# TensorE products into an unread PSUM bank ahead of four kinds of wait in a two-layer hybrid decoder step

## The chip, the cores and the metric

One NeuronCore of a Trainium2 chip runs the whole program. The metric is the time of one execution in microseconds (us); for the kernel before it is the median of three runs. A profile was taken of one further execution.

## The reference, cut to what matters

The program computes one step of a two-layer decoder trunk for 512 prompt tokens and 8 sequences of 4 sample tokens, 544 columns in all, with a model width of 1024. Layer 0 has an HGRN2 mixer (gated linear recurrence), layer 1 a gated DeltaNet mixer with a causal convolution over four taps; a squared-ReLU MLP of width 4096 follows each. Everything is float32. Of layer 1, which the change touches:

```python
q = l2norm(q) * DK ** -0.5; k = l2norm(k)
beta = sigmoid(b); g = -exp(A_log) * softplus(a + dt_bias)
M = eye + where(strict, beta * kk * decay, 0)          # a unit lower triangle per chunk
u = triangular_solve(M, v * beta); w = triangular_solve(M, k * (beta * exp(G)))
# then, chunk by chunk: v_new = u - w S; o = qg S + (qk * decay) v_new; S = gl S + kd^T v_new
```

The dense projections around it are `h @ w_in` and `o @ w_out`. Nothing in the reference answers to the products that the change adds.

## The kernel before, in words

**Layout.** Activations are held transposed, features on 128 partitions, tokens along the free axis, in eight tiles of 128 x 544 (`xT`). A dense projection is a chain of "units": a unit multiplies eight 128 x 128 weight tiles by eight activation tiles. Each of its eight steps (`tiles`, line 494) issues six products of 272 columns, since weight and activation are split into a high and a low part of type float32r and three of the four cross terms are kept; they go to the PSUM tensor `pj`. All other TensorE work is in plain float32 and goes to `rr`, a PSUM tensor of four banks: transposes (`tr`, line 541), sums over features by a matrix of ones (`sum_features`, line 523, two products of 128 x 272) and the recurrence itself.

**Order of the work.** Each engine runs one program in its own order and waits on semaphores. TensorE (PE) has no other order than the one written out in the block from line 490 on. The first mixer, its output projection and its MLP come first. Then the second mixer begins with a prologue: `first_unit(U_AB, "n2")` projects the 16 gate columns, `gdn_pre` (line 684) waits for VectorE and ScalarE to turn them into decay factors and transposes the result (line 689), and the loop at line 941 walks the list `GDN_SLOTS` for head 0: `more(n)` (from `head_projections`, line 513) issues n steps of that head's four projection units, then `gdn_prepare(slot, 0)` issues the small products of the slot. 16 steps go ahead of slot L0 and two ahead of each slot in `GDN_FILLED`, until all 32 are used, which is the case from slot L5 on. Slot L5 (line 718) sums the squares of k, L6 (721) forms k k^T, C0 (727) sums the squares of q, C1 (731) forms k q^T and C2 (737) transposes three small columns. Each of them waits for VectorE or ScalarE. `gdn_first_inverse` (line 744) transposes the first inverse; then 16 steps of the next head's projections follow (line 945).

**The heads.** `gdn_rec` (line 761) runs once for each of eight heads. It builds the inverse of M by doubling: for m = 2, 4, ..., 64 it forms a product `x{m}` (line 783 for m = 2, else line 787), waits for ScalarE's copy of it, forms `dt{m}` (line 823), waits for VectorE to put that in place (`pred{m}`, line 2062), transposes the result (`tr{m}`, line 833, counted under line 543) and waits for ScalarE's copy `tt{m}` (line 1385) before the next level. Steps of the next head's projections (`more`) and its slots are put between these. At m = 16 the wait for `tt8` stands at line 778, right behind slot L3 of the next head (line 715). VectorE's own list there is long: three convolution taps (line 1881), a negative absolute value (1665) and the decay of the sample states (1654) lie ahead of `pred16`. Head 7 prepares no next head. Heads are counted from 0.

Of the kernel before, what the change touches and what calls it, by code (L numbers as in the profile page):

```python
# [14 lines left out]
P = 128  # L15
# [6 lines left out]
HALF = T // 2  # L22
# [113 lines left out]
def fixed(eng, value):  # L136

    return value if isinstance(value, int) else eng.to_reg(value)


def build(nc, x_prompt, x_sample, state_hgrn, state_gdn, state_conv, norm_mix, norm_mlp, norm_final, hgrn_w_in,
          hgrn_lb, hgrn_out_norm, hgrn_w_out, gdn_w_in, gdn_conv_w, gdn_A_log, gdn_dt_bias, gdn_out_norm, gdn_w_out,
          mlp_w_up, mlp_w_down, const_f, const_u, y_prompt, y_sample, hgrn_p, hgrn_s, gdn_p, gdn_s, conv_p, conv_s):
    with ExitStack() as ctx:
        def sb(name, shape, dt=F32):
            return ctx.enter_context(nc.sbuf_tensor(name, shape, dt))
# [5 lines left out]
        xT = sb("xT", [P, KT, T])  # L152
# [13 lines left out]
        ones = sb("ones", [P, P])  # L166
# [61 lines left out]
        rr = ctx.enter_context(nc.psum_tensor("rr", [P, 4, 512], F32))  # L228
# [262 lines left out]
        def _(pe):  # L491
            mm = nc.tensor.matmul
# [30 lines left out]
            def sum_features(bank, src, start=True, stop=True):  # L523

                for b in range(2):
                    last = mm(rr[:, bank + b, 0:HALF], ones[:], src[:, b * HALF:(b + 1) * HALF], start=start, stop=stop)  # L526
                return last
# [13 lines left out]
            def tr(out, in_):  # L541
                n = in_.shape[0]
                return nc.tensor.transpose(out, in_, cf[0:n, C_EYE:C_EYE + n])  # L543
# [63 lines left out]
            def hgrn_rec(h, more):  # L607
# [73 lines left out]
                t.did(sum_features(2, hg["sq"]), "ss")  # L681
                more(3)

            def gdn_pre():
                v, s, t = st["gp"]
                pe.wait_ge(v.sem, v.after("turn", 0))
                pe.wait_ge(s.sem, s.after("eg", 0))
                for c in range(NC):
                    tr(rr[:, 2, c * P:(c + 1) * P], gt4[:, c * P:(c + 1) * P])
                t.did(tr(rr[0:TS, 3, 0:P], gt4[:, TP:T]), "cols")  # L690

            def held(*waits):

                values = [(steps.sem, fixed(pe, steps.after(name, h))) for steps, name, h in waits]
                pe.wait_ge(c_in, 16 * N_CONST)
                for sem_, value in values:
                    pe.wait_ge(sem_, value)

            def gdn_prepare(slot, h):

                v, s, t = st["ga"]
                nQ, nK, work = gd["nQ"], gd["nK"], gd["work"]
                if slot == "L1":
                    loaded = fixed(pe, h * 16 + 16)
                    pe.wait_ge(c_in, 16 * N_CONST)
                    pe.wait_ge(cv_in, loaded)
                    for g in range(3):
                        last = tr(rr[:, 3, SVN + g * 32:SVN + g * 32 + XW * NSEQ], cin[:, g, :])
                    t.did(last, "cin")
                if slot in ("L3", "L4"):  # L710
                    g, name = (0, "gb") if slot == "L3" else (1, "bb")
                    pe.wait_ge(s.sem, s.after("G" if g else "hist", h))
                    pe.wait_ge(v.sem, v.after("gsel", h))
                    for b in range(2):
                        last = mm(rr[:, 2 + b, 0:HALF], ones[32 * g:32 * (g + 1), :],
                                  work[32 * g:32 * (g + 1), b * HALF:(b + 1) * HALF], start=True, stop=True)
                    t.did(last, name)
                if slot == "L5":
                    pe.wait_ge(s.sem, s.after("sqk", h))
                    t.did(sum_features(2, work), "ssk")  # L720
                if slot == "L6":
                    pe.wait_ge(v.sem, v.after("kb", h))
                    for c in range(NC):
                        cols = slice(c * P, (c + 1) * P)
                        mm(rr[:, 2 + c // 2, c % 2 * P:(c % 2 + 1) * P], nK[:, cols], work[:, cols], start=True, stop=True)  # L725
                    t.did(mm(rr[0:TS, 2, 2 * P:2 * P + TS], nK[:, TP:T], work[:, TP:T], start=True, stop=True), "kk")
                if slot == "C0":
                    pe.wait_ge(s.sem, s.after("sqq", h))
                    pe.wait_ge(v.sem, v.after("kkd", h))
                    t.did(sum_features(2, gd["G"]), "ssq")  # L730
                if slot == "C1":
                    pe.wait_ge(v.sem, v.after("qn", h))
                    for c in range(NC):
                        cols = slice(c * P, (c + 1) * P)
                        mm(rr[:, 2 + c // 2, c % 2 * P:(c % 2 + 1) * P], nK[:, cols], nQ[:, cols], start=True, stop=True)  # L735
                    t.did(mm(rr[0:TS, 3, 2 * P:2 * P + TS], nK[:, TP:T], nQ[:, TP:T], start=True, stop=True), "qk")
                if slot == "C2":
                    held((v, "qkd", h))
                    for g in range(3):
                        n = XW * (NSEQ + 1)  # L740
                        last = tr(rr[0:n, 2 + g // 2, g % 2 * P:(g % 2 + 1) * P], cstash[:, g, :])
                    t.did(last, "stash")
# [12 lines left out]
            def gdn_finish(h):  # L755

                _, s, t = st["gf"]
                pe.wait_ge(st["gr"][1].sem, st["gr"][1].after("sq", h))
                t.did(sum_features(2, gd["sq"]), "ss")

            def gdn_rec(h, prev, nxt, more, later):
# [3 lines left out]
                K, qe, A, NL, Tm, Tt, X, kdT, vT, VN = (gd[n] for n in ("K", "qe", "A", "NL", "Tm", "Tt", "X", "kdT",  # L765
                                                                        "vT", "VN"))


                for n, m in enumerate(LEVELS[1:]):
                    smp = m in SLEVELS  # L770
                    if n == 0:
                        pe.wait_ge(sa.sem, sa.after("tm0", h))
                        if prev is not None:
                            pe.wait_ge(v.sem, v.after("sn1", prev))
                        if prev is not None:
                            gdn_finish(prev)
                    else:
                        pe.wait_ge(s.sem, s.after(f"tt{LEVELS[n]}", h))
                    if n == 0:
                        for c in range(NC):  # L780
# [3 lines left out]
                    else:  # L784
                        pe.wait_ge(mixed.sem, mixed.after(f"m{m}", h))
                        for q in range(NC // 2):
                            last = mm(rr[:, 0, q * P:(q + 1) * P], NLm[n % 2][:, q * P:(q + 1) * P], earlier(Tm, q, m),  # L787
                                      start=True, stop=True)
                    if smp:
                        last = mm(rr[0:TS, 1, 0:TS // 2], NL[0:TS, TP:T], first_half(Tm[0:TS, TP:T], m),  # L790
                                  start=True, stop=True)
                    t.did(last, f"x{m}")
                    if m == 4 and nxt is not None:
                        pe.wait_ge(v.sem, v.after("vb", h))
                        gdn_prepare("L1", nxt)
                    if m == 32 and nxt is not None:
                        held((s, "rs", h))
                        gdn_prepare("L4", nxt)
                    if m == 64 and nxt is not None:
                        held((s, "vns", h))  # L800
                        gdn_prepare("L5", nxt)
# [23 lines left out]
                    if smp:  # L825
                        last = mm(rr[0:TS, 1, TS // 2:TS], Tt[0:TS, TP:T], X[0:TS, TP // 2:T // 2],
                                  start=True, stop=True)
# [37 lines left out]
                for q in range(NC // 2):  # L865
                    last = mm(rr[:, 0, 256 + q * P:256 + (q + 1) * P], X[:, q * P:(q + 1) * P], later_ends(Tt, q),
                              start=True, stop=True)
# [68 lines left out]
            mlp(U_MLP0, "n1", "up0")  # L936
            first_unit(U_AB, "n2")
            gdn_pre()
            more = head_projections(U_GIN, 0)
            pe.wait_ge(st["gp"][1].sem, st["gp"][1].after("cols", 0))  # L940
# [3 lines left out]
            gdn_first_inverse(0, (st["ga"][1], "cout", 0))  # L944
            head_projections(U_GIN, 1, 0, 2)(2 * KT)
            gdn_rec(0, None, 1, head_projections(U_GIN, 1, 2, 4), head_projections(U_GIN, 2, 0, 2))
            with pe.Fori(1, H - 2) as h:
                gdn_rec(h, h - 1, h + 1, head_projections(U_GIN, h + 1, 2, 4), head_projections(U_GIN, h + 2, 0, 2))
# [5 lines left out]
            def first_two(n):  # L954
                n = min(n, (6 if n == 1 else 12) - taken[0])
                more(n)
                taken[0] += n

            gdn_rec(H - 2, H - 3, H - 1, head_projections(U_GIN, H - 1, 2, 4), first_two)
            held_back = [28]  # L960

# [530 lines left out]
        def _(dve):  # L1492
# [36 lines left out]
            for i in (0, 2):  # L1529
                after(t, "t", i)  # L1530
                v.did(cp(xT[:, :, i * P:(i + 1) * P], rr[:, 2:4, :].rearrange("p a (k n) -> p (a k) n", n=P)), "copy")
            v2, _, t2 = st["xs"]
            after(t2, "t", 0)
            v2.did(cp(xT[:, :, TP:T], rr[:, 2, 0:KT * TS].rearrange("p (k n) -> p k n", n=TS)), "copy")
# [324 lines left out]
            def gdn_prepare(slot, h):  # L1859
# [27 lines left out]
                def silu(name, row, dst):  # L1887

                    after(s, f"{name}sig", h)
                    for (o, a), (_, b) in list(zip(by_position(dst, pr[:, row, 0:T]), by_position(dst, ng[:, row, 0:T])))[0:2]:  # L1890
                        tt(o, a, b, ALU.mult)
                    v.did(tt(blocks(dst[:, TP:T], SLEN), blocks(pr[:, row, SB0:XPW], SROW)[:, :, 0:SLEN],
                             blocks(ng[:, row, SB0:XPW], SROW)[:, :, 0:SLEN], ALU.mult), f"{name}s")
# [353 lines left out]
```

## Time and profile before

| | us |
|---|---|
| median of 3 runs | 1838.19 |
| lowest and highest run | 1837.34, 1839.09 |
| the profiled execution | 1838.72 |
| its span, first to last instruction | 1836.9 |
| mean granted TensorE clock in the span | 0.959 of full speed |

In the profile, PE is TensorE's matmul side and PEld its weight loads; DVE is VectorE, ACT ScalarE, POOL GpSimd. A granted clock of 1.00 is the 2.4 GHz level, 0.50 the 1.2 GHz level. The end of a product is modelled and includes the time in which it drains, so products issued back to back overlap in the rows: their spacing is shorter than the length of one. A row of the timeline joins instructions of one line that follow each other; the bracket at its end is the idle time of the engine ahead of it and the instruction that ended it.

### The profile page before, as it was taken

To read this page: it belongs to the slowest core of one execution; us is meant where nothing else is said; L and a number is where in the kernel's file an instruction comes from. 1 tells how busy PE (TensorE), PEld (TensorE's weight loads), DVE (VectorE), ACT (ScalarE), POOL (GpSimd) and SP (SyncE) were. 2 spreads that over 40 slices of the span, in tenths; PEclk is the share of its full clock that TensorE was granted. 3 is DMA by queue.
4 is the path that set the end of the run, shared out by engine and by line. 5 is a ranking of instruction groups with operands and counts; after the bars stand their busy time and mean duration, and the time that the engine had idled before them with its cause. 6 is when DMAs were issued, how large, how long until landed. Compare 5 with 4: busy or idle time off the path is not lost.

```text
span 1836.9 us, 33057 instructions
## 1 busy us (share of the span) xinstructions
PE 1704.1 (93%) x12555; PEld 1606.0 (87%) x12555; DVE 1101.8 (60%) x2177; ACT 700.0 (38%) x1220; POOL 38.8 (2%) x85
## 2 busy tenths in 40 slices
PE   6999999899999999977998998999898999999996
PEld 6988888899999999976887787777777999999996
DVE  5888888865343443556568667766765434344444
ACT  5555555543122222224345445444533312122222
POOL 0000000000000000000100100000010000000000
PEclk9999999999999999988899998999998999999997
DMA  5232222223323233221121221121122223323321
GB/s 167 63 89 81 70 81 70 77 84 92 88 86 92 82 89 92 70 69 36 48 61 36 60 60 35 48 60 48 35 75 65 84 85 89 92 81 91 90 70 49
DMA packets 257849, 135.07 MB, mean 74 GB/s; under 512 B 6746, under 2 KB 256180, under 8 KB 257780
## 3 DMA queue, kind: packets, MB, share of 16 engines
q1 hardware_dynamic: 219920, 113.35, 22.0%
q10 hardware_dynamic: 37860, 20.76, 3.9%
q8 instruction: 49, 0.80, 0.2%
q14 instruction: 20, 0.16, 0.0%
HBM read 122.09 MB, written 12.00 MB: 73 GB/s over the span
## 4 chain that ended last, share of the span: by engine, by line
PE 42%; DVE 6%; issue 3%; ACT 2%; ACTq 0%; DVEq 0%
PE pj L505 31%; PE rr L543 3%; PE rr L526 1%; DVE pr L1881 1%; PE rr L787 1%; PE rr L807 1%; PE rr L823 1%; PE rr L895 1%; DVE w_lo L1540 1%; DVE ws L2062 0%; ACT ng L1245 0%; DVE ws L1648 0%; PE rr L725 0%; PE rr L735 0%; DVE ng L1665 0%
## 5 line engine op out<-in xcount | busy, mean ns | idle before, releaser
L505 PE MATMUL pj<-xh,w_hi 128*128 128x272 f32 x2064 | 461.6, 306 | 23.4 <-DVE w_lo L1540 13.0
L1017 ACT ACTIVATE w_hi<-w_raw 128x1024 fp32r<-128x1024 f32 x211 | 222.4, 1054 | 581.9 <-PE pj L505 565.3
L505 PE MATMUL pj<-xh,w_lo 128*128 128x272 f32 x2064 | 434.8, 293 | 0.0
L505 PE MATMUL pj<-xl,w_hi 128*128 128x272 f32 x2064 | 434.6, 293 | 0.0
L505 PEld LDWEIGHTS pj<-xh,w_hi 128*128 128x128 f32 x2064 | 330.7, 194 | 52.8 <-issue 29.5
L505 PEld LDWEIGHTS pj<-xl,w_hi 128*128 128x128 f32 x2064 | 333.1, 193 | 0.0
L505 PEld LDWEIGHTS pj<-xh,w_lo 128*128 128x128 f32 x2064 | 331.3, 194 | 0.0
L1540 DVE TENSOR_TENSOR w_lo<-w_raw,w_hi 128x1024 fp32r<-128x1024 f32 x211 | 256.8, 1217 | 41.1 <-ACT w_hi L1017 41.0
L505 PE MATMUL pj<-oh,w_hi 128*128 128x272 f32 x1254 | 266.6, 294 | 14.6 <-DVE w_lo L1540 10.4
L505 PE MATMUL pj<-oh,w_lo 128*128 128x272 f32 x1254 | 262.1, 291 | 0.0
L505 PE MATMUL pj<-ol,w_hi 128*128 128x272 f32 x1254 | 261.3, 290 | 0.0
L505 PEld LDWEIGHTS pj<-oh,w_hi 128*128 128x128 f32 x1254 | 199.5, 191 | 18.9 <-DVE w_lo L1540 11.5
L505 PEld LDWEIGHTS pj<-ol,w_hi 128*128 128x128 f32 x1254 | 200.0, 191 | 0.0
L505 PEld LDWEIGHTS pj<-oh,w_lo 128*128 128x128 f32 x1254 | 198.5, 191 | 0.0
L2153 DVE TENSOR_TENSOR ws<-pj,rstd 128x544 f32<-128x544 f32 x64 | 46.4, 724 | 188.2 <-PE pj L505 180.0
L2165 DVE TENSOR_TENSOR xT<-xT,pj 128x544 f32<-128x544 f32 x48 | 34.6, 721 | 167.9 <-PE pj L505 167.9
L543 PE MATMUL rr<-cf,ws 128*128 128x128 f32 (+2 forms) x440 | 73.3, 306 | 21.2 <-DVE ws L2062 10.8
L543 PEld LDWEIGHTS rr<-cf,ws 128*128 128x128 f32 (+2 forms) x440 | 53.6, 152 | 35.4 <-DVE ws L2062 14.0
L482 POOL COPY ws<-ws 128x128 f32<-128x128 f32 x80 | 38.4, 513 | 1327.2 <-DVE ws L1968 872.1
L1881 DVE SCALAR_TENSOR_TENSOR pr<-xp,hcw,pr 128x568 f32<-128x568 f32 x72 | 58.2, 809 | 7.3 <-ACT pr L1240 5.8
L1669 DVE SCALAR_TENSOR_TENSOR ng<-pr,ng 128x544 f32<-128x544 f32 (+1 forms) x56 | 40.6, 726 | 32.1 <-ACT ng L1105 19.0
L526 PE MATMUL rr<-ws,ones 128*128 128x272 f32 x148 | 44.4, 424 | 11.6 <-ACT ws L1295 3.8
(317 smaller groups left out, 1959.9 us busy)
## 6 DMA issues: line engine op xcount, KB each, us to landing
w_raw<-in_mlp_w_up_dram SPq DMA_DIRECT2D x64, 512.0 KB, 4.1
w_raw<-in_mlp_w_down_dram SPq DMA_DIRECT2D x64, 512.0 KB, 3.9
w_raw<-in_hgrn_w_in_dram SPq DMA_DIRECT2D x32, 512.0 KB, 4.2
w_raw<-in_gdn_w_in_dram SPq DMA_DIRECT2D x32, 512.0 KB, 4.0
out_dram<-S ACTq DMA_DIRECT2D x16, 512.0 KB, 3.3
S<-in_state_hgrn_dram ACTq DMA_DIRECT2D x8, 512.0 KB, 4.1
w_raw<-in_hgrn_w_out_dram SPq DMA_DIRECT2D x8, 512.0 KB, 3.8
S<-in_state_gdn_dram ACTq DMA_DIRECT2D x8, 512.0 KB, 4.0
```

The source lines that it names most:

```text
L482: last = nc.gpsimd.tensor_copy(interleaved(NLm[n % 2], m, odd), pair_half(gd["NL"][:, 0:TP], m, odd, odd))
L505: last = mm(pj[:, s, b, 0:HALF], w[:, s, k, :], v[:, k, b * HALF:(b + 1) * HALF], start=(k == 0 and a == 0), stop=(k == end - 1 and a == 2))
L526: last = mm(rr[:, bank + b, 0:HALF], ones[:], src[:, b * HALF:(b + 1) * HALF], start=start, stop=stop)
L543: return nc.tensor.transpose(out, in_, cf[0:n, C_EYE:C_EYE + n])
L787: last = mm(rr[:, 0, q * P:(q + 1) * P], NLm[n % 2][:, q * P:(q + 1) * P], earlier(Tm, q, m), start=True, stop=True)
L807: last = mm(rr[:, 1, 2 * b * SLEN:2 * (b + 1) * SLEN], S0[:, b, :], both, start=True, stop=True)
L1017: f(w_hi[:, c % SPLIT, 0:n], w_raw[:, slot, 0:n], ACT.Copy).then_inc(w_high, 1)
L1540: tt(w_lo[:, c % SPLIT, 0:n], w_raw[:, c % RAW, 0:n], w_hi[:, c % SPLIT, 0:n], ALU.subtract).then_inc(w_low, 1)
L1669: return stt(out=ng[:, row, 0:w], in0=pr[:, row, 0:w], scalar=0.0, in1=ng[:, row, 0:w], op0=ALU.min, op1=ALU.subtract)
L1881: v.did(stt(out=pr[:, row, 0:YW], in0=xp[:, row, j:j + YW], scalar=hcw[:, j, g:g + 1], in1=pr[:, row, 0:YW], op0=ALU.mult, op1=ALU.add), f ...
L2153: tt(halves(B[:, k % 2]), computed(U, r, k), halves(rstd[:]), ALU.mult).then_inc(unit_out, 1)
L2165: tt(halves(xT[:, k]), halves(xT[:, k]), computed(U, g * (2 * KT), KT + k), ALU.add).then_inc(unit_out, 1)
```

## The change

It adds a helper `keep_busy`, which issues n float32 products of the matrix of ones with a source that lies ready, each of which starts and stops its own accumulation in a given bank of `rr`. No instruction reads what they write. It is called at four kinds of place on PE: in `gdn_pre` ahead of the two waits (44 products of 272 columns, bank 3); in the prologue's slots L5, L6 and C1, of head 0 alone (16, 12 and 8 products of 272 columns, bank 0); and in each of the eight heads at level m = 16, ahead of the wait for `tt8` (4 products of 256 columns, bank 0). No other engine's program changes, and no wait or DMA is added or moved.

```diff
+            def keep_busy(bank, src, n):
+
+                for _ in range(n):
+                    mm(rr[:, bank, 0:src.shape[1]], ones[:], src, start=True, stop=True)
+
             def gdn_pre():
                 v, s, t = st["gp"]
+                keep_busy(3, xT[:, 0, 0:HALF], 44)
                 pe.wait_ge(v.sem, v.after("turn", 0))
                 pe.wait_ge(s.sem, s.after("eg", 0))
...
                 nQ, nK, work = gd["nQ"], gd["nK"], gd["work"]
+                if isinstance(h, int) and h == 0 and slot in ("L5", "L6", "C1"):
+                    keep_busy(0, xT[:, 0, 0:HALF], 16 if slot == "L5" else 12 if slot == "L6" else 8)
                 if slot == "L1":
...
                     else:
+                        if m == 16:
+                            keep_busy(0, A[:, 0:2 * P], 4)
                         pe.wait_ge(s.sem, s.after(f"tt{LEVELS[n]}", h))
```

## Rows read from the trace of the kernel before

**Rows 1.** The page, span in 40 slices: granted clock in tenths of full speed.
```profile
PEclk9999999999999999988899998999998999999997
```
**Rows 2.** Stretches of set length: busy time (instructions) per engine, granted clock, DMA share, GB/s.
```profile
810.80:824.40 13.60, 5.46 (x23) 5.01 (x24) 4.99 (x10) 3.99 (x11) 0.00 (x0) 0.50 0.15 39
...
855.20:879.00 23.80, 14.42 (x51) 10.85 (x52) 16.90 (x41) 12.48 (x23) 1.22 (x4) 0.50 0.18 47
974.70:978.00 3.30, 3.30 (x17) 3.30 (x17) 3.19 (x5) 1.46 (x3) 1.05 (x2) 0.50 0.00 0
...
1107.80:1114.50 6.70, 5.27 (x25) 4.88 (x24) 5.27 (x14) 2.61 (x8) 0.64 (x1) 0.50 0.00 0
...
1305.80:1309.00 3.20, 0.76 (x7) 0.55 (x5) 3.13 (x7) 0.31 (x1) 0.21 (x1) 1.00 0.00 0
1309.20:1312.50 3.30, 3.30 (x15) 3.07 (x15) 1.89 (x9) 2.23 (x6) 0.00 (x0) 0.50 0.00 0
```
**Rows 3.** Timeline of PE, 805 to 825 us: start, us, line, operation, count, [idle before, releaser].
```profile
805.77 1.08 PE L526 MATMUL rr<-ws,ones 128*128 128x272 f32 x4
...
807.19 0.42 PE L505 MATMUL pj<-xh,w_lo 128*128 128x272 f32 x2
818.50 1.30 PE L543 MATMUL rr<-cf,gt 128*128 128x128 f32 x5 [10.89 <-ACT gt L1221]
820.23 0.82 PE L505 MATMUL pj<-xh,w_hi 128*128 128x272 f32 x2 [0.43 <-ACT gcol L1224]
```
**Rows 4.** Timeline of PE, 851 to 880 us.
```profile
851.61 0.41 PE L505 MATMUL pj<-xh,w_lo 128*128 128x272 f32 x2
855.78 2.18 PE L526 MATMUL rr<-ws,ones 128*128 128x272 f32 x4 [3.76 <-ACT ws L1295]
861.36 2.08 PE L725 MATMUL rr<-ws 128*128 128x128 f32 x8 [3.40 <-DVE ws L1941]
...
869.05 2.08 PE L735 MATMUL rr<-ws 128*128 128x128 f32 x8 [2.25 <-DVE ws L1953]
...
874.37 1.28 PE L543 MATMUL rr<-cf,ws 128*128 128x128 f32 x5 [1.20 <-DVE ws L1982]
875.58 0.82 PE L505 MATMUL pj<-xh,w_hi 128*128 128x272 f32 x2
```
**Rows 5.** PE's waits, 880 to 1440 us: total us, times, longest.
```profile
PE rr L787 <- ACT ws L1385: 10.7, 7, 1.6
...
PE rr L787 <- DVE rt L2093: 0.6, 1, 0.6
```
**Rows 6.** Timeline of PE around level 16, heads 1 (from 971) and 6 (from 1301).
```profile
971.55 1.18 PE L715 MATMUL rr<-ws,ones 32*128 32x272 f32 x4
974.28 0.94 PE L787 MATMUL rr<-ws 128*128 128x128 f32 x4 [1.56 <-ACT ws L1385]
...
979.48 0.66 PE L543 MATMUL rr<-cf,ws 128*128 128x128 f32 x4 [0.97 <-DVE ws L2062]
...
980.83 0.40 PE L787 MATMUL rr<-ws 128*128 128x128 f32 x2
...
1303.90 0.71 PE L787 MATMUL rr<-ws 128*128 128x128 f32 x4 [1.48 <-ACT ws L1385]
...
1306.15 0.41 PE L505 MATMUL pj<-xh,w_lo 128*128 128x272 f32 x2
1309.09 1.11 PE L543 MATMUL rr<-cf,ws 128*128 128x128 f32 x4 [2.52 <-DVE ws L2062]
...
1311.58 0.84 PE L787 MATMUL rr<-ws 128*128 128x128 f32 x3
```
**Rows 7.** The chain that ended last, in order of time, head 0 around level 16.
```profile
911.15 0.82 DVE pr L1881
...
912.66 1.22 DVE S L1654
```
**Rows 8.** The instructions of line 526: duration ns min/median/max, first and last start.
```profile
L526 PE MATMUL rr<-ws,ones x148: 390/393/821, 31.5 to 1814.6; 128*128 128x272 f32 x148
```

## The prediction

> **What bounds the kernel now.** I read the page's clock line first, then stretches of set length, then PE's timeline and waits where the clock is low, then the chain that ended last.
>
> The clock line is at 9 or more but for the second mixer [rows 1]. There the half level (0.50) holds for 13.6 us around the gates' wait and for 23.8 us at the end of the prologue, and once or twice in each head [rows 2]. Ahead of the first stretch PE idles 10.89 us for the gates, and its projections then start at the half level at 820.23 [rows 3]. Ahead of the second it idles 3.76 us for the squares of k, then 3.40 and 2.25 us [rows 4]. In the heads, `x16` waits some 1.5 us for `tt8` in heads 0 to 6, together 10.7 us, and 0.6 us in head 7 [rows 5]. The reader is to see two sorts of low clock: one where PE's products are next on the path (the prologue's projections), and one where another engine is. At level 16 the chain runs through VectorE's taps of 0.82 us and the decay of 1.22 us, not through PE [rows 7].
>
> **One added product.** The nearest row is the same instruction: `sum_features` has two calls of 128 x 272 float32, and its row has four matmuls, 1.08 us in all [rows 3]. So a call is two records. The last one is 0.39 long [rows 8], so the spacing is (1.08 - 0.39) / 3 = 0.23 us, and a call takes 0.46 us at the full level. One of 256 columns takes 0.46 x 256/272 = 0.43. At the half level four records take 2.18 [rows 4], twice as much.
>
> **The gates' wait.** 44 calls take 44 x 0.46 = 20.2 us. They begin behind the last projection step (807.19 + 0.42, its drain aside, 807.4) and end at 827.6. Today the transposes start at 818.50, so PE comes 9.1 us late. Gained: the five transposes go at the full level, 0.65 instead of 1.30, so the projections start at 828.7 instead of 820.23, 8.5 us later. Today they run at the half level from 820.23 to 824.4 [rows 2, 3]; these 4.2 us would be 2.1. Behind them all engines wait for PE's first unit (VectorE is busy 4.99 of 13.60 us there [rows 2], all of it ahead of the wait), so nothing hides the delay. Net **+6.4**; bounds +5.4 (a gap between transposes and projections that shrinks) and +8.5 (nothing regained). ScalarE and VectorE stand still meanwhile, and SyncE's weight loads behind them, which nobody needs earlier.
>
> **The prologue's three slots.** L5: 16 calls, 7.3 us, begin at 852.0 and end at 859.3 instead of 855.78, 3.5 us late; the sum at the full level takes 1.1 us less, lag 2.4. L6: 12 calls, 5.5 us, against a wait of 3.40: lag 2.4 + 2.1 = 4.5, less 1.2 for k k^T at the full level, 3.3. The next sum has no calls ahead of it and takes 1.1 less, lag 2.2. C1: 8 calls, 3.7 us, against 2.25: lag 3.6, less 1.2 for k q^T, 2.4. VectorE's work up to 874.37 is as long as before. The transposes there take 0.64 less and the 3.4 us of projections up to 879.0 that ran at the half level take 1.7 less: lag 0.1. But in the last 3 us ahead of the projections PE is left with three short transposes. Head 6 shows what follows: 0.76 us busy of 3.2 at the full level, then 3.3 us at the half level [rows 2]. I take the same here, 1.6 lost. Net **+1.7**; bounds 0 and +3.4 (two such stretches).
>
> **The heads.** Four calls take 1.73 us and end where `x16` starts now (behind the sums from 971.55 they end at 974.3; it starts at 974.28 [rows 6]). In heads 0 to 6 that is no delay, and 0.1 us would be hidden behind VectorE's taps. In head 7 the calls overrun a wait of 0.6 us [rows 5] plus a drain of some 0.15: **+1.0** (bounds 0 and 1.0).
>
> What does the clock give back there? Head 1 goes from `x16` to the transposes of `pred16` in 979.48 - 974.28 = 5.20 us with 3.3 of them at the half level; head 6 in 1309.09 - 1303.90 = 5.19 at the full level [rows 2, 6]. Nothing: VectorE ends last. But from the transposes to `x32` head 1 (full) takes 980.83 - 979.48 = 1.35 and head 6 (half) 1311.58 - 1309.09 = 2.49. A low stretch is free while VectorE works and costs 1.1 us once it comes later. Calls ahead of `x16` take away the first idle time, but the second stays: behind `dt16` PE waits 2.52 us in head 6 [rows 6]. So the low stretch doesn't go in all heads; in some it moves from the free place to the dear one. Heads 3 (low from 1107.8 to 1114.5 [rows 2]) and 6 pay already. I take two more of the other five, **+2.0**; bounds -2.2 (heads 3 and 6 freed too) and +5.5 (all five).
>
> The Trainium skill says otherwise (TensorE: Matmul & The Clock Gate, section on HAM oscillation): a throttled stretch costs its length times 1 - 1.2/2.4, so half of it. By that each of seven heads would gain at least 1.6 us here. Heads 1 and 6, equal within 0.01 us, do not bear it out at this place.
>
> **The sum.** 6.4 + 1.7 + 1.0 + 2.0 = 11.1 us on the profiled execution of 1838.72, which is 0.5 above the median: 1849.3 as a median. What this measurement can tell from no change is about 0.2%, 3.7 us.
>
> **The rivals.**
>
> *The low stretches simply go*, in heads 3 and 6 too, and none comes back ahead of the next head's projections: 6.4 + 0 + 1.0 - 2.2 = 5.2, 1843.4. For it: the calls are back to back. Against: the second idle time at level 16. Chance 0.15.
>
> *The low stretches move to the dear place in all heads* and stay for twice the time in the prologue: 6.4 + 3.4 + 1.0 + 5.5 = 16.3, 1854.5. Chance 0.15.
>
> *The half level costs half its time everywhere, and the change is faster.* The stretches aimed at are 13.6 + 23.8 us and, with one per head like those of heads 1, 3 and 6, about 27 in seven heads: 64 us, so 32 gained. Against that stand PE's overruns at full speed: 9.1 + 3.5 + 2.1 + 1.4 + 1.0 = 17.1. That is 15 us faster, 1823. It decides as soon as more than 17.1 of the 32 are on the path; by the sums above it is 2.8 at the gates, some 6 in the slots and at most 2.2 in the heads. Chance 0.07. It is the rule of the Trainium skill named above, carried through.
>
> *The change does not do what it says*: a call is one record, 0.23 us. Then 44 calls (10.1 us) and the slots' 3.7, 2.8 and 1.8 fit into 10.89, 3.76, 3.40 and 2.25; the gates gain 2.8 and the slots some 6: 1829. The count of the four matmuls speaks against it [rows 3]. Chance 0.03.
>
> *The overrun at the gates is swallowed* by a wait that I don't see, and the rest cancels: 1838 to 1841. Chance 0.05.
>
> **How the numbers follow.** The forecast has 0.55 and is 1849.3. All low bounds give 5.4 + 0 + 0 - 2.2 = 3.2, all high ones 8.5 + 3.4 + 1.0 + 5.5 = 18.4; with the cases of 1843.4 and 1854.5 inside, the range is 1842 to 1857. Faster: 0.07 + 0.03 = 0.10; same 0.05; slower 0.85.
>
> **What would show it.** The added line under the gates should show 88 matmuls over some 20 us, the transposes of line 543 at about 827.6 with no idle time ahead of them, the wait for ScalarE there gone, and the clock at 1.00 from 807 on. The sum of line 526 in the prologue should start about 3.5 us later relative to the work ahead of it and take 1.08. In heads 0 to 6 the distance from `x16` to the transposes of `pred16` should stay 5.2 us, and PE's wait on line 2062 there grow to some 2.5 us. Transposes at 818 to 819 us would make the forecast wrong at its largest term; a distance well under 5.2 us would make the reading of the heads wrong; a low clock right behind the 44 calls would mean that such products do not hold it.

## The result, and the profile after

The median is 1850.03 us (1845.17 to 1851.22, five runs) against 1838.19 (1836.86 to 1841.49): the ratio that the runs give is 1.0055 (the two medians alone give 1.0064), with a 95% interval of 1.0041 to 1.0070, so 0.4 to 0.7% slower. The profiled execution took 1850.03, its span 1848.2 us. The mean granted clock rose from 0.959 to 0.972, and the time rose too. Below, a "low stretch" is a time in which the granted clock is 0.50.

The page's clock line has lost the run of eights at the prologue that [rows 1] show:

```profile
PEclk9999999999999999999999999998998999999997
```

PE's timeline at the gates' wait answers to [rows 3] (start, us, line, operation, count, idle before and its releaser; the added products are line 687):

```profile
807.59 20.33 PE L687 MATMUL rr<-xT,ones 128*128 128x272 f32 x88
...
827.76 0.71 PE L543 MATMUL rr<-cf,gt 128*128 128x128 f32 x5
...
828.90 0.52 PE L505 MATMUL pj<-xh,w_hi 128*128 128x272 f32 x2 [0.43 <-ACT gcol L1234]
```

The 44 calls are 88 matmuls, as the count of four for two calls had said, one every (827.76 - 807.59) / 88 = 0.23 us. The wait for ScalarE of 10.89 us has no row any more: when PE comes to it, the gates are long ready. The transposes begin 9.3 us later than in [rows 3], the projections 8.7; 0.14 us of each is the start of the norm's sum, 805.91 against 805.77.

The end of the prologue, same view, answers to [rows 4]:

```profile
858.63 7.49 PE L687 MATMUL rr<-xT,ones 128*128 128x272 f32 x32
...
865.96 1.08 PE L526 MATMUL rr<-ws,ones 128*128 128x272 f32 x4
866.88 5.66 PE L687 MATMUL rr<-xT,ones 128*128 128x272 f32 x24
872.38 1.05 PE L733 MATMUL rr<-ws 128*128 128x128 f32 x8
...
875.56 3.83 PE L687 MATMUL rr<-xT,ones 128*128 128x272 f32 x16
879.23 1.05 PE L743 MATMUL rr<-ws 128*128 128x128 f32 x8
...
883.43 1.27 PE L543 MATMUL rr<-cf,ws 128*128 128x128 f32 x5 [1.52 <-DVE ws L1992]
884.64 0.82 PE L505 MATMUL pj<-xh,w_hi 128*128 128x272 f32 x2
```

The sum of slot L5 and the products of L6 and C1 now take half as long (1.08, 1.05 and 1.05 us) and have no idle time ahead of them, but each starts late. Behind the last of them PE idles again, the last transposes take 1.27 us, as long as before, and the projections at 884.64 start with a length of 0.82, the half level's. Stretches of set length show the clock there (busy time and instructions of PE, PEld, DVE, ACT, POOL; granted clock; DMA share; GB/s), as [rows 2] did:

```profile
807.60:827.70 20.10, 20.10 (x90) 16.67 (x89) 7.43 (x14) 5.49 (x13) 0.00 (x0) 1.00 0.12 34
858.70:882.80 24.10, 21.29 (x104) 17.47 (x102) 17.11 (x38) 13.85 (x25) 0.68 (x3) 1.00 0.12 27
882.90:889.60 6.70, 6.17 (x27) 5.77 (x28) 3.13 (x15) 1.76 (x4) 0.44 (x2) 0.50 0.23 66
```

In the heads, PE's timeline around level 16 of head 1, and behind it the late part of head 5, answer to [rows 6]:

```profile
982.24 1.18 PE L723 MATMUL rr<-ws,ones 32*128 32x272 f32 x4
983.35 1.99 PE L687 MATMUL rr<-ws,ones 128*128 128x256 f32 x8
985.18 0.61 PE L797 MATMUL rr<-ws 128*128 128x128 f32 x4
...
990.09 0.66 PE L543 MATMUL rr<-cf,ws 128*128 128x128 f32 x4 [2.36 <-DVE ws L2072]
...
991.44 0.62 PE L797 MATMUL rr<-ws 128*128 128x128 f32 x4
...
1254.93 1.05 PE L797 MATMUL rr<-ws 128*128 128x128 f32 x4
1255.92 2.18 PE L723 MATMUL rr<-ws,ones 32*128 32x272 f32 x4
...
1263.48 0.61 PE L797 MATMUL rr<-ws 128*128 128x128 f32 x4
```

Head 1 goes through level 16 at the full level. Its `x16` comes 0.2 us later behind the start of the sums than in [rows 6] (985.18 - 982.24 = 2.94 against 2.73), and from there it is 4.91 us to the transposes instead of 5.20: what is lost ahead of `x16` is idle time less behind it, and the idle time ahead of the transposes has grown from 0.97 to 2.36. In head 5 the low clock comes where it hurts: from `x32` at 1254.93 to `x64` at 1263.48 are 8.55 us, against 6.1 in heads that keep the clock. PE was busy in all of that low stretch:

```profile
1255.00:1261.70 6.70, 6.70 (x25) 5.53 (x25) 3.84 (x10) 5.54 (x12) 0.00 (x0) 0.50 0.25 73
```

Where the time went can be read off three starts in PE's timeline: the norm's sum of line 526 ahead of the gates (805.77 before, 805.91 after), `x2` of head 0 (889.25; 899.04) and `x2` of head 7 (1347.72; 1358.08), and from there to the second sample update `dSs1` of head 7. The same three distances are given for every kernel below; "prologue" is from the norm to head 0.

| kernel | median, us | ratio to before, interval | profiled execution | prologue | heads 0-6 | head 7 |
|---|---|---|---|---|---|---|
| before | 1838.19 | | 1838.72 | 83.48 | 458.47 | 44.01 |
| the change | 1850.03 | 1.0055 (1.0041 to 1.0070) | 1850.03 | 93.12 | 459.04 | 44.89 |
| gates only, 44 | 1842.76 | 1.0033 (1.0019 to 1.0047) | 1841.30 | 90.23 | 454.97 | 43.99 |
| slots only | 1839.20 | 1.0011 (0.9998 to 1.0024) | 1844.43 | 86.56 | 459.31 | 43.98 |
| heads only | 1840.10 | 1.0013 (1.0002 to 1.0024) | 1836.00 | 84.16 | 455.75 | 44.90 |
| gates only, 23 | 1835.96 | 0.9998 (0.9985 to 1.0010) | 1836.93 | 81.14 | 457.62 | 44.00 |
| slots fitted | 1836.95 | 0.9999 (0.9988 to 1.0010) | 1835.69 | 80.85 | 457.37 | 44.00 |
| slots covered | 1836.60 | 0.9986 (0.9975 to 0.9998) | 1836.71 | 79.64 | 459.38 | 43.99 |
| heads, two fills | 1836.26 | 0.9990 (0.9979 to 1.0002) | 1836.56 | 83.69 | 455.05 | 43.99 |
| all fitted | 1831.84 | 0.9964 (0.9949 to 0.9979) | 1827.47 | 77.91 | 451.92 | 44.01 |

The ratios go by runs on the experiment's own chip, where the kernel before had medians of 1837.57 (30 runs) and 1837.78 (34), with single runs from 1832.2 to 1841.7. The three parts of the change, 1.0033, 1.0011 and 1.0013, add up to 1.0057 there, against 1.0055 for the whole. But such a spread hides a part of 2 us, so the parts are read from the three distances as well, each from one profiled execution. Head 7 repeats best, 43.98 to 44.01 in the eight kernels that leave it alone; the prologue is 83.48, 83.69 and 84.16 in the three that leave it alone; heads 0 to 6 vary most, and the next section shows why. The profiled execution can lie anywhere among the runs: with the slots only it was the slowest of twelve, with the heads only it was 4 us below its median. Up to 1.8 us of the difference between two such executions lies outside the three distances, where the kernels do not differ.

### The profile page after: what moved, and what is told of

The parts are those of the page before. It is cut to its first block, busy times and chain, and to the rows that moved or that the text cites. A ratio compares the mean times of both kernels' runs of the same rounds, so it can differ in the third digit from the quotient of the medians.

```text
span 1848.2 us, 33505 instructions
## 1 busy us (share of the span) xinstructions
PE 1739.5 (94%) x12779; PEld 1637.7 (89%) x12779; DVE 1102.2 (60%) x2177; ACT 700.6 (38%) x1220; POOL 37.2 (2%) x85
## 4 chain that ended last, share of the span: by engine, by line
PE 80%; DVE 11%; issue 4%; ACT 4%; ACTq 0%; DVEq 0%; DMA 0%
PE pj L505 61%; PE rr L543 4%; PE rr L687 2%; PE rr L526 2%; DVE w_lo L1550 2%; PE rr L623 1%; DVE pr L1891 1%; PE rr L668 1%; PE rr L661 1%; PE rr L797 1%; PE rr L817 1%; PE rr L833 1%; PE rr L905 1%; DVE ws L1581 1%; PE rr L743 0%
## 5 line engine op out<-in xcount | busy, mean ns | idle before, releaser
L1444 ACT ACTIVATE oh<-ws 128x544 fp32r<-128x544 f32 x64 | 42.3, 661 | 28.9 <-DVE ws L2165 28.9
```

Of the source, the lines that this page charges most:

```text
L1444: s.did(f(oh[:, k], B[:, 2 + k % 2], ACT.Copy), f"hi{k}")
```

## The experiments

**Gates only.** The change without its calls in the slots and the heads.

```diff
-                if isinstance(h, int) and h == 0 and slot in ("L5", "L6", "C1"):
-                    keep_busy(0, xT[:, 0, 0:HALF], 16 if slot == "L5" else 12 if slot == "L6" else 8)
-                        if m == 16:
-                            keep_busy(0, A[:, 0:2 * P], 4)
```

> Only the 44 products at the gates' wait. Overrun theory: the added products end at 827.8, 9.2 us after the gates are ready; with the clock kept at 1.00 the net is +6.6 us, so 6 to 7 us over the kernel before. Rival (half-level time costs half of itself, the overrun is swallowed by slack behind it): the low stretch of 13.6 us goes and 2 to 7 us are gained.

Measured: prologue +6.75 us, ratio 1.0033, so +6 us. The overrun is paid in full. It is read best where PE next waits for weights, in the kernel before and here:

```profile
836.47 0.52 PE L505 MATMUL pj<-xh,w_hi 128*128 128x272 f32 x2 [2.08 <-DVE w_lo L1540]
...
842.50 0.52 PE L505 MATMUL pj<-xh,w_hi 128*128 128x272 f32 x2 [2.08 <-DVE w_lo L1546]
```

Behind the norm's sum (805.77 before, 805.14 here) that is 30.70 us and 37.36, so 6.66 us later, and VectorE has moved with PE: the wait for it is 2.08 us in both. In the whole change the distance is 37.36 as well. Behind this place the present kernel has a low stretch of 3.4 us that the whole change lacks; its 1.3 us come back in shorter waits and in the next low stretch but for 0.1.

**Slots only.** The change without its calls at the gates and in the heads.

```diff
-                keep_busy(3, xT[:, 0, 0:HALF], 44)
-                        if m == 16:
-                            keep_busy(0, A[:, 0:2 * P], 4)
```

> Only the 16, 12 and 8 products in the slots L5, L6 and C1 of the prologue. Overrun theory: between +0.1 us, if the clock stays up behind C1, and +3.4 us, if PE's projections of the next head run at the half level for two stretches as they did with the whole change; I take +3. Rival (half of the 23.8 us of low clock is gained, less 7 us of overrun): 5 us faster than the kernel before.

Measured: prologue +3.08 us. The long low stretch ahead of the next head's projections goes from 23.9 us to 6.8, and this part still loses: all three groups overrun their waits, and the stretch that is left lies on the next head's projections. With the gates the two parts make 6.75 + 3.08 = 9.83, against 9.64 for the whole change. The median's +2 us is no contradiction, its interval reaches from -0.4 to +4.4.

**Heads only.** The change without its calls at the gates and in the slots.

```diff
-                keep_busy(3, xT[:, 0, 0:HALF], 44)
-                if isinstance(h, int) and h == 0 and slot in ("L5", "L6", "C1"):
-                    keep_busy(0, xT[:, 0, 0:HALF], 16 if slot == "L5" else 12 if slot == "L6" else 8)
```

> Only the 4 products at level 16 of each head. Theory (VectorE ends last at level 16, and a low stretch costs only where it falls behind pred16): head 7 pays 0.9 us, the others between -2 and +4 us together depending on where the low stretches fall; 0 to +4 us. Rival (each low stretch of 3.4 us at level 16 costs half of it): four to seven of them go and 7 to 12 us are gained, less 0.9.

Measured: head 7 +0.89 us, ratio 1.0013. None of the seven other heads has a low stretch at level 16; head 4 has one of 6.8 us from `x32` on instead, and takes 67.58 us where it took 65.27 before. In this execution heads 0 to 6 are 2.7 us shorter than before, but the runs have the part as a whole 0.4 to 4.4 us slower. This and the kernel with the gates only make the cleanest pair of the study, for in the latter a low stretch begins around `x16` and ends ahead of `pred16` in each of heads 0 to 6. PE around level 16 of head 1 with the gates only (`x16` is line 793), and the clock there:

```profile
980.43 1.22 PE L793 MATMUL rr<-ws 128*128 128x128 f32 x4 [1.56 <-ACT ws L1391]
...
985.54 0.66 PE L543 MATMUL rr<-cf,ws 128*128 128x128 f32 x4 [0.88 <-DVE ws L2068]
...
986.90 0.62 PE L793 MATMUL rr<-ws 128*128 128x128 f32 x4
```
```profile
980.50:983.80 3.30, 3.30 (x15) 3.30 (x16) 3.19 (x5) 1.46 (x3) 1.54 (x2) 0.50 0.00 0
```

and the same head with the heads' calls only (`x16` is line 794):

```profile
973.95 0.61 PE L794 MATMUL rr<-ws 128*128 128x128 f32 x4
...
978.87 0.66 PE L543 MATMUL rr<-cf,ws 128*128 128x128 f32 x4 [2.36 <-DVE ws L2069]
...
980.22 0.61 PE L794 MATMUL rr<-ws 128*128 128x128 f32 x4
```
```profile
970.00:981.00 11.00, 8.64 (x57) 7.35 (x56) 9.83 (x23) 4.79 (x13) 1.10 (x2) 1.00 0.00 0
```

`x16` takes 1.22 us in the one and 0.61 in the other, and the head as a whole, from `x2` to the next `x2`, takes 65.25 us in both. Heads 0, 3, 5 and 6 agree within 0.02 us too; heads 2 and 4 differ by longer low stretches elsewhere. PE at double speed buys idle time: 2.36 us ahead of the transposes instead of 0.88, both released by VectorE's `pred16`. Half of a low stretch is not what it costs here; nothing is.

**The gates' wait, filled but not overrun.** 23 calls instead of 44, nothing else.

```diff
-                keep_busy(3, xT[:, 0, 0:HALF], 44)
+                keep_busy(3, xT[:, 0, 0:HALF], 23)
```

> Only the gates, with 23 products instead of 44: 46 matmuls of 0.229 us, 10.5 us, which fit into the 10.9 us wait. Overrun theory: the transposes start at 818.5 as before, go at the full level, and the projections start at 819.7 and run at the full level: 2.4 to 2.8 us faster than the kernel before. If something else held the prologue (the rival in which the overrun is swallowed), this would change nothing, 0 within 1 us.

PE's timeline at the gates (no row lies between the first two), where it next waits for weights, and the clock behind that:

```profile
808.48 10.71 PE L687 MATMUL rr<-xT,ones 128*128 128x272 f32 x46
819.54 0.74 PE L543 MATMUL rr<-cf,gt 128*128 128x128 f32 x5 [0.35 <-ACT gt L1227]
...
835.10 0.52 PE L505 MATMUL pj<-xh,w_hi 128*128 128x272 f32 x2 [2.08 <-DVE w_lo L1546]
```
```profile
836.20:839.50 3.30, 3.30 (x17) 3.00 (x16) 0.00 (x0) 0.95 (x6) 0.00 (x0) 0.50 0.59 160
```

Measured: prologue -2.34 us. The five transposes take 0.74 us instead of 1.30, the projections behind them run at the full level, and the wait for weights ends 28.30 us behind the norm's sum (806.80), 2.40 earlier than before. That is what the gates give. Behind it lies a low stretch that the kernel before does not have there. It costs PE 1.3 us; 0.65 of that is made up by a shorter wait for ScalarE ahead of L5, and 0.6 because the next low stretch ends earlier against the projections, so that the -2.34 of the whole prologue agrees partly by chance. 21 calls more, at 0.46 us each, are 9.6 us; less the 0.35 us that is idle here they make 9.3, and the two prologues differ by 9.1. The median is 1.6 us below the one of before, and the runs alone could not tell this from no change.

**The slots, fitted.** 8, 9 and 5 calls instead of 16, 12 and 8, nothing else.

```diff
-                    keep_busy(0, xT[:, 0, 0:HALF], 16 if slot == "L5" else 12 if slot == "L6" else 8)
+                    keep_busy(0, xT[:, 0, 0:HALF], {'L5': 8, 'L6': 9, 'C1': 5}[slot])
```

> Only the slots, with 8, 9 and 5 products instead of 16, 12 and 8, so that they end before the waits do. Theory: nothing is late any more; k k^T and the sum of the squares of q at the full level give 1.1 us each, the wait of k k^T itself stays (VectorE's taps end last there), and the projections behind still start at the half level: from the gates' norm to x2 of head 0 about 81.3 us against 83.5 before, so 2 us faster. Rival (half of the low clock counts): the 23.8 us of low clock give 8 to 10 us.

Measured: prologue -2.63 us, 80.85 against the 81.3 expected; the median -0.8, within the interval. The end of the prologue, and the clock ahead of and behind its last transposes:

```profile
870.65 0.49 PE L543 MATMUL rr<-cf,cstash 128*27 128x128 f32 x3 [1.97 <-DVE ws L1907]
872.66 1.27 PE L543 MATMUL rr<-cf,ws 128*128 128x128 f32 x5 [1.52 <-DVE ws L1989]
873.87 0.82 PE L505 MATMUL pj<-xh,w_hi 128*128 128x272 f32 x2
```
```profile
868.60:872.40 3.80, 0.57 (x5) 0.24 (x3) 3.70 (x11) 1.85 (x4) 1.05 (x4) 1.00 0.25 47
872.50:875.80 3.30, 3.14 (x13) 2.75 (x14) 2.77 (x14) 1.76 (x4) 0.07 (x1) 0.50 0.37 106
```

PE is busy 0.57 of 3.80 us, and the half level follows, onto the projections.

**The slots, fitted and covered.** The same, with products ahead of three more waits.

```diff
-                    keep_busy(0, xT[:, 0, 0:HALF], {'L5': 8, 'L6': 9, 'C1': 5}[slot])
+                    keep_busy(0, xT[:, 0, 0:HALF], {'L5': 8, 'L6': 9, 'C0': 2, 'C1': 5, 'C2': 4}[slot])
...
+                if isinstance(h, int) and h == 0:
+                    keep_busy(0, xT[:, 0, 0:HALF], 3)
                 pe.wait_ge(v.sem, v.after("tt1", h))
```

> As the fitted slots, and 2 products ahead of C0's wait, 4 ahead of C2's and 3 ahead of the first inverse's, so that no idle time is left ahead of the next head's projections. Theory: these now run at the full level: from the norm to x2 about 79.2 us against 83.5 before, 2 us less than with the fitted slots alone; 4 us faster than the kernel before. If the low stretch came for another reason than the idle time ahead of it, it would stay and this would equal the fitted slots.

The last transposes, the first projections and the clock in the same place:

```profile
873.40 0.79 PE L543 MATMUL rr<-cf,ws 128*128 128x128 f32 x5
874.12 0.52 PE L505 MATMUL pj<-xh,w_hi 128*128 128x272 f32 x2
```
```profile
868.60:872.40 3.80, 3.80 (x22) 2.94 (x22) 3.77 (x9) 1.80 (x4) 0.31 (x2) 1.00 0.11 14
873.00:885.00 12.00, 11.85 (x94) 11.39 (x92) 5.00 (x19) 2.82 (x5) 0.31 (x2) 1.00 0.18 43
```

Measured: prologue -3.84 us, ratio 0.9986. No low stretch is left at the end of the prologue. The 3.3 us of half level in the fitted slots were worth 80.85 - 79.64 = 1.2 us; here PE is next, and the larger part of half their length is really paid.

**Two fills in the heads.** The 4 products at level 16, in heads 0 to 6 alone, and 5 more ahead of the wait for `pred16`, in bank 1, whose last content ScalarE has copied by then.

```diff
-                        if m == 16:
+                        if m == 16 and nxt is not None:
                             keep_busy(0, A[:, 0:2 * P], 4)
...
                     more(1)
+                    if m == 16 and nxt is not None:
+                        keep_busy(1, A[:, 0:2 * P], 5)
                     pe.wait_ge(v.sem, v.after(f"pred{m}", h))
```

> Only heads 0 to 6: the 4 products ahead of tt8 and 5 more (bank 1) ahead of the wait for pred16, where PE was idle for 2.5 us. Theory: no low stretch at level 16 in any head, so x32 always comes 1.36 us behind the transposes of pred16, and heads 0 to 6 take 453.4 us plus 1.5 for each long low stretch at dSs0, about 455 against 458.5 in the profile of before; 2 to 4 us faster than it, 0 to 3 in the median. Rival (half of each stretch counts): 7 x 1.7 = 12 us faster.

PE in head 1 from the second fill to `x32`:

```profile
977.65 2.32 PE L687 MATMUL rr<-ws,ones 128*128 128x256 f32 x10
980.16 0.66 PE L543 MATMUL rr<-cf,ws 128*128 128x128 f32 x4 [0.19 <-DVE ws L2071]
...
981.51 0.62 PE L794 MATMUL rr<-ws 128*128 128x128 f32 x4
```

Measured: no low stretch at level 16 in any head; in all seven `x32` follows the transposes by 1.35 to 1.36 us, as 981.51 - 980.16 does here. Heads 0 to 6 take 455.05 us, against 458.47 in the profile of before; the median is 1.5 us lower and the interval of the ratio (0.9979 to 1.0002) just takes in no change. Half of seven stretches, 12 us, is refuted. Of the 3.4 us between the two profiles, heads 3 and 6, which paid at level 16 before, give 1.8; the other 1.6 is head 5, whose low stretch between the sample updates is 3.4 us long here and 6.8 before.

**All of it, fitted.** 23 at the gates, the covered slots, the two fills.

> All together, fitted: 23 products at the gates, the covered slots, two fills in heads 0 to 6, none in head 7. Theory: the parts add up, -2.4 at the gates, -4.3 in the slots, -2 in the heads: about 8 to 9 us faster than the kernel before, 76.8 us from the norm to x2. Rival (half of all low clock): 25 us faster.

Measured: 1831.84 us, ratio 0.9964, so 4 to 9 us faster than the kernel before and the fastest here. The prologue gave -5.57 us, 1.1 less than expected; a low stretch of 3.4 us lay 29 us behind the norm in this execution, where PE waits 2.1 us for weights, as in the two kernels with calls at the gates only. Heads 0 to 6 took 451.92. Two of these heads show what is left over: between the two sample updates `dSs0` and `dSs1` (lines 909 and 915), head 0 kept the clock and head 1 did not.

```profile
938.34 1.12 PE L909 MATMUL rr<-ws,kdTs 32*128 32x512 f32 x2 [1.45 <-DVE Sp L1676]
...
942.32 1.10 PE L915 MATMUL rr<-ws,kdTs 32*128 32x512 f32 x2
...
1002.07 1.12 PE L909 MATMUL rr<-ws,kdTs 32*128 32x512 f32 x2 [1.45 <-DVE Sp L1676]
...
1007.57 1.10 PE L915 MATMUL rr<-ws,kdTs 32*128 32x512 f32 x2
```
```profile
936.00:943.00 7.00, 5.55 (x33) 4.03 (x33) 5.22 (x13) 3.78 (x8) 0.00 (x0) 1.00 0.35 88
...
1003.50:1006.80 3.30, 3.30 (x17) 3.30 (x16) 1.64 (x2) 1.66 (x4) 0.00 (x0) 0.50 0.13 23
```

3.98 us against 5.50: here one low stretch costs 1.5 us, because 18 projection products stand between the two updates and PE is next throughout. Heads 0 to 6 of the kernel before all have it: there the distance is 5.50 to 5.54 us, and 6.83 and 7.04 in heads 2 and 5, where the low stretch is 6.8 us long. Products ahead of `dSs0` were not tried; in the order of the program none of the four banks seemed free at that point.

## Why the prediction was right

**The main term held.** "44 calls take 44 x 0.46 = 20.2 us", from four matmuls of a sum that does the same, came out as 20.2 (827.76 - 807.59). The net of 6.4 us was 6.66 at the wait for weights, with the gates alone and in the whole change: the projections started 8.5 us late, as forecast, and the full level gave them back 1.9 instead of 2.1. That nothing hides the delay is what the 2.08 us of that wait show, the same with 0, 23 and 44 calls.

**The slots were sized low.** The step said 1.7 us within 0 to 3.4; 3.08 was measured alone in the profile, and the runs (-0.4 to +4.4) can't tell the two apart. The lags were right: k k^T was forecast 4.5 us late by the slots and came at 872.38, 11.0 behind [rows 4], of which 6.6 are the gates' and 0.1 the earlier program's, so 4.3; the last transposes were forecast 2.4 us late and came 2.3. What failed is what follows them, "the transposes there take 0.64 less" and "I take the same here, 1.6 lost", from a low stretch of 3.3 us. It was 6.7 long and began ahead of the transposes, which took 1.27 us, as before; 5.1 us of projections ran at the half level, where 3.4 did before. In the fitted slots it was 3.3 long. One such stretch or two: the working had both as bounds, and took the shorter. What makes a low stretch the one length or the other is not shown.

**The heads: the mechanism right, the count not settled.** VectorE ends last at level 16 in heads 0 to 6 of every kernel; the low stretch is free ahead of `pred16` and dear behind it. The forecast of +2.0 was +0.57 in the profiled pair. Heads 0, 3 and 5 pay after the change, heads 3 and 6 before, so one more and not two; but what one pays differs. The row from the transposes to `x32` gave 1.1 us; a part of that comes back in the next level, and a long low stretch from `x32` on, which no row of before showed, cost 2.4 in head 5. The step also looked at level 16 alone: the long low stretch between the sample updates, which cost heads 2 and 5 some 1.5 us each before, came in head 2 only, and that took 1.5 off. Over kernels this term is the luck of where the stretches fall: heads 0 to 6 took 455.0 to 459.4 us in the executions where the calls at level 16 are as in the kernel before. That single runs of one kernel differ by 9 us fits with it, but only one execution of each kernel was profiled.

**Head 7** was forecast at +1.0 and paid 0.88. Over many executions heads 0 to 7 together, forecast at +3.0, cost 2.4 (0.4 to 4.4) by the runs of the heads only.

**The sum.** In the profiled pair the parts are 6.66 + 2.98 + 0.57 + 0.88 = 11.1 us, the forecast to a tenth. That it fits so closely is luck: the slots were 1.3 us over their term and heads 0 to 6 were 1.4 under theirs.

**The rivals.** That half of each low stretch counts was refuted at level 16 (65.25 us with and without it) and wherever a part was tested against it: the slots only, 5 us faster by it, came out 2 slower by the median, and all fitted, 25 faster by it, came out 6. The granted clock rose from 0.959 to 0.972 and the time with it. In the Trainium skill (TensorE: Matmul & The Clock Gate, section on HAM oscillation) it is the rule: a throttled stretch costs its length times 1 - 1.2/2.4. Where PE is next the runs come close to it, 1.5 us for 3.3 us between the sample updates, 1.2 for 3.3 at the projections. Taken so, it gives what a low stretch costs PE, not what PE costs the kernel. The rival in which the low stretches simply go fails at 882.90 and in heads 0, 3 and 5. Of the one in which the stretches move to the dear place in all heads and stay twice as long in the prologue, the half on the prologue came true; in the heads two of seven had one at the transposes of level 16 and a third had one from `x32` on. A call is two matmuls, and no wait swallowed the overrun.

## What to carry to other kernels

Before work is put into an idle engine to hold its clock, multiply it out with the duration of the same instruction form in the trace, matmuls counted as rows and not as calls in the source, and keep it under the wait: what is over is paid one for one where that engine is next, less what the higher clock gives back. Then ask of each low stretch who ends last in it. A stretch under another engine's work is free, and taking it away can be followed by one in a place where it is not, as in head 4 with the heads' calls only. Covering a part of the idle time can pay (the fitted slots gave 2.6 us); covering all of it up to the dense work gave 1.2 more.

## What the runs showed that was not expected

- Eight matmuls of 256 columns behind sums with 32 rows took 985.18 - 983.35 = 1.83 us and began 1.11 us behind the start of the four sum matmuls, whose spacing of 0.23 would have had them there at 0.92: with that, `x16` came 0.2 to 0.3 us late in heads 0 to 6, where the prediction had it on time. It cost nothing, since VectorE ends last there.
- The same 3.3 us at the half level cost 0, 1.2 and 1.5 us in three places of this program.
- Some low stretches are twice as long, 6.7 us; that, and not the occurrence of one, made the slots' term 1.4 us larger than forecast. PE was idle for the first 0.5 us of the one at the end of the prologue, but busy all through the one of head 5, so idle time in its first part is not what it takes, and the reason stays open.
